# Five pairs of weight blocks by Strassen's seven products in a decoder's memory stage

## What is computed

```python
proj = h @ w_in
qkv, b, a, qm, z = jnp.split(proj, [3 * WIDTH_B, ...])
...
om = mem_attend(qm.reshape(B, T, MEM_HEADS, HEAD_DIM), mem_k, mem_v).reshape(B, T, WIDTH_MEM)
branch = jnp.concatenate([o, om], axis=-1) * jax.nn.silu(z)
return branch @ w_out, new_conv, S.astype(sdt)
```

## Time and profile before

| | before |
|---|---|
| median of 3 runs (their extremes) | 2191.96 us (2190.51 to 2194.2) |
| the profiled execution's own time | 2194.7 us |
| its span, first to last instruction | 2192.7 us |
| PE busy, share of the span | 2154.7 us, 98% |
| DVE, ACT, POOL busy | 938.3, 663.8, 456.4 us |

### The profile page before, as it was taken

The page is one execution under the profiler, slowest core; times in us unless marked ns, Lnnn a source line. Parts: engine busy times, 40 slices in busy tenths (PEclk is TensorE's granted clock), DMA queues, the critical chain, the costliest instruction groups (busy, mean ns, idle before and its releaser), DMA issues.

```text
span 2192.7 us, 46735 instructions
## 1 busy us (share of the span) xinstructions
PE 2154.7 (98%) x19630; PEld 1531.5 (70%) x19630; DVE 938.3 (43%) x2431; ACT 663.8 (30%) x1589; POOL 456.4 (21%) x642
## 2 busy tenths in 40 slices
PE   8999999999999999999999999999999999999998
PEld 6888888888888876544567667676676666665444
DVE  5234354354344444321355555555555233333252
ACT  4122321312222131311234434444344344442101
POOL 0522241242123205000032322322322110020000
PEclk9999999999999999999999999999999999999999
DMA  7412211212221166666012212122110173114451
GB/s 227 154 42 64 81 30 41 78 43 67 58 59 42 35 212 227 213 207 212 13 62 93 70 74 83 67 79 80 60 53 14 40 273 97 39 59 148 136 168 53
DMA packets 210278, 210.99 MB, mean 96 GB/s; under 512 B 14262, under 2 KB 181654, under 8 KB 209151
## 3 DMA queue, kind: packets, MB, share of 16 engines
q1 hardware_dynamic: 198070, 148.27, 22.4%
q0 software_dynamic: 12000, 59.73, 7.1%
HBM read 179.56 MB, written 68.23 MB: 113 GB/s over the span
## 4 chain that ended last, share of the span: by engine, by line
PE 50%; DVE 0%; ACT 0%; issue 0%; POOL 0%; DVEq 0%
PE bank L2088 19%; PE bank L2802 8%; PE bank L3292 7%; PE bank L2146 4%; PE bank L2162 4%; PE bank L2144 2%; PE bank L2154 1%; PE bank L2818 1%; PE bank L2827 1%; PE bank L3270 1%; PE bank L3303 0%; PE bank L2177 0%; PE bank L3199 0%; PE bank L3176 0%; PE bank L2810 0%; PE bank L3186 0%
## 5 line engine op out<-in xcount | busy, mean ns | idle before, releaser
L884 PE MATMUL bank<-arena 128*128 128x256 f32 (+1 forms) x2688 | 631.7, 386 | 0.0
L884 PEld LDWEIGHTS bank<-arena 128*128 128x128 f32 x2688 | 494.5, 190 | 75.3
L2088 PE MATMUL bank<-arena 128*128 128x352 f32 x1296 | 469.2, 474 | 0.1
L2088 PEld LDWEIGHTS bank<-arena 128*128 128x128 f32 x1296 | 214.0, 190 | 58.1 <-ACT arena L2309 0.6
L2802 PE MATMUL bank<-arena 128*128 128x352 f32 x576 | 176.4, 459 | 0.0
L3292 PE MATMUL bank<-arena 128*128 128x512 f32 x360 | 167.5, 599 | 0.0
L2146 PEld LDWEIGHTS bank<-arena 128*128 128x128 f32 x864 | 125.5, 192 | 36.7 <-issue 0.3
L2802 PEld LDWEIGHTS bank<-arena 128*128 128x128 f32 x576 | 106.6, 190 | 53.3
L2162 PEld LDWEIGHTS bank<-arena 32*32 32x32 f32 x7680 | 78.8, 105 | 91.6 <-issue 39.8
L1338 POOL TENSOR_TENSOR arena<-arena 128x272 f32<-128x272 f32 (+1 forms) x48 | 31.5, 656 | 507.6 <-ACT arena L1058 487.6
L2146 PE MATMUL bank<-arena 128*128 128x128 f32 x864 | 131.3, 278 | 0.2 <-ACT arena L2329 0.2
(11 more groups left out here) (426 smaller groups left out, 2720.2 us busy)
## 6 DMA issues: line engine op xcount, KB each, us to landing
arena<-in_w_in_a SPq DMA_DIRECT2D x48, 512.0 KB, 5.1
arena<-in_w_in_b SPq DMA_DIRECT2D x40, 512.0 KB, 4.1
arena<-in_cache_win_k SPq DMA_DIRECT2D x48, 256.0 KB, 5.1
arena<-in_cache_win_v SPq DMA_DIRECT2D x48, 256.0 KB, 3.6
out<-arena SPq DMA_DIRECT2D x40, 256.0 KB, 3.3
arena<-in_w_mem_kv SPq DMA_DIRECT2D x16, 512.0 KB, 8.0
arena<-in_cache_mem_k SPq DMA_DIRECT2D x32, 256.0 KB, 4.1
arena<-in_cache_mem_v SPq DMA_DIRECT2D x32, 256.0 KB, 3.4
```

The lines of the kernel that those rows point to most:

```text
L884: m = nc.tensor.matmul(o[:, 0:hi - lo], w, y, start=k == 0 and i in (0, 1, 3, 5), stop=k == KH - 1, skip_group_check=i in (2, 4, 6))
L2088: m = nc.tensor.matmul(bank[j % 3][:, 0:PART], ring.slots[:, (B1 + b) % RING, k, :], part_in(k, part_), start=k == 0, stop=k == KD - 1)
```

## The change

Blocks 5 to 14 become five pairs (some blocks change places so that pairs fit). For a pair, the two weight blocks are the columns and the two halves of the contraction the rows of a 2 x 2 matrix; a quarter of the tokens (264) and the next quarter make the other matrix. One *task* is one pair with one half of the tokens: seven products of four matmuls of 264 columns each (28 *units*; the plain form has eight such products). There are ten tasks, two a pair. Their 280 units and the eight of block 15's first piece are spread over the 32 turns by `m_at`: 168 over the first 15 turns, 120 over the other 17.

POOL forms the four sums of tokens of each task (264 x 4 columns each, into buffers that the next task overwrites), the four sums of weights of each pair (128 x 4 columns) and one difference of products a task, and the six later gate multiplications stand between them. DVE reads each product out of PSUM (a copy or an addition; two instructions for the seventh), in its turn between `turned(x-1)` and `normed(x)`. ACT's work on products is the silu, in place, of both blocks when a task is done. The buffers lie where five of the `w_out_b` blocks were to lie, so these are loaded when the last product has been read.

```diff
@@ -206,8 +206,8 @@
         c += (s * P, H * E + (HB + s) * P, H * E + 2 * s * P, H * E + (2 * s + 1) * P)[i]
         return w_in_b[0][:, c:c + P]
 
-    M_BLOCKS = [(0, 0), (0, 1), (0, 2), (0, 3), (1, 0), (1, 1), (1, 2), (2, 0), (2, 1), (1, 3), (3, 0), (3, 1),
-                (2, 2), (2, 3), (3, 2), (3, 3)]
+    M_BLOCKS = [(0, 0), (0, 1), (0, 2), (0, 3), (1, 0), (1, 1), (1, 2), (1, 3), (2, 2), (2, 0), (2, 1),
+                (3, 0), (3, 1), (2, 3), (3, 2), (3, 3)]
@@ -2762,15 +2762,57 @@
...
+    WO_LATE = (0, 1, 2, 3, 4)
+    QUART = TOK // 4
+    HALVES = ((0, QUART, 2 * QUART), (2 * QUART, 3 * QUART, 4 * QUART))
+    tk2, tk3, tk4, tk1 = (sb[:, o:o + TOK].rearrange("p (k c) -> p k c", c=QUART)
+                          for o in (WO_B[0], WO_B[3], ZM[0] + TOK, WO_B[2]))
+    ws2, ws1, ws4 = (sb[:, o:o + KH * P].rearrange("p (k c) -> p k c", c=P)
+                     for o in (WO_B[0] + TOK, qs_at, qs_at + KH * P))
+    s1w, u2b, u3b = (sb[:, WO_B[4] + QUART * n:WO_B[4] + QUART * (n + 1)] for n in range(3))
+    tpd, tpv, tpp, tws, ttk, tz = (sem(f"m_{n}") for n in (
+        "product_done", "product_read", "third_less", "weight_sums", "token_sums", "pair_gates"))
+    a_of = lambda t: bank[2 * (t % 2)]
+    c_of = lambda t: bank[2 - 2 * (t % 2)]
+    PAIR0, NPAIRS = 5, 5
+    NTASKS = 2 * NPAIRS
     (p2, pr2d, sc2, scr2, mx2, ex2, nm2, tn2, tr2, pv2, or2, zo2, nct, ncr) = (sem(f"m_{n}") for n in (
         "piece_done", "piece_read", "scores", "scores_read", "max", "exp", "normed", "turned", "turned_read",
         "values", "values_read", "gated", "conv_turned", "conv_read"))
     nco = stored["conv"]
-    NP2 = 3 * len(M_BLOCKS)
+    NP2 = IN_B + 6
     FIRST_M, LAST_M = IN_B + 3, 2
-    beside = lambda x: range(FIRST_M + x * (NP2 - FIRST_M - LAST_M) // (8 * H),
-                             FIRST_M + (x + 1) * (NP2 - FIRST_M - LAST_M) // (8 * H))
-    queries_read = lambda s: 3 * (M_AT[(s, 1)] + 1) - IN_B
+    munits = [("product", t, i, k) for t in range(NTASKS) for i in range(NPROD) for k in range(KH)]
+    munits += [("piece", FIRST_M, 0, k) for k in range(KD)]
+    MID = 6 * NPROD * KH
+    m_at = lambda x: x * MID // 15 if x < 15 else MID + (x - 15) * (len(munits) - MID) // (8 * H - 15)
+    beside = lambda x: munits[m_at(x):m_at(x + 1)]
+    ended_m = lambda x: [(kind, t, i) for kind, t, i, k in beside(x) if k == (KD if kind == "piece" else KH) - 1]
+    block_of = lambda j: j // 3 if j < FIRST_M else len(M_BLOCKS) - 1
+    pair_of = lambda b: (b - PAIR0) // 2
+    def block_home(s, i, cs):
+        return (mq_of(s) if i == 0 else zm_of(s) if i == 1 else zo_of(s, i - 2))[:, cs]
...
@@ -2779,7 +2821,7 @@
                 sp.dma_start(wo_b(k), w_out_b[0][k * P:(k + 1) * P]).then_inc(w_out_in[1], 16)
 
         readout(sp, NG_ - 1, "ot")
-        w_load(range(6))
+        w_load((5,))
         sp.wait_ge(ncr, 6)
...
         sp.wait_ge(or2, 8 * (H - 1))
         w_load(range(9, 11))
         ring.load(sp, B2 + 16)
+        sp.wait_ge(tpd, NPROD * NTASKS)
+        sp.wait_ge(tpv, 8 * NTASKS)
+        w_load(WO_LATE)
...
+        def product(t, i, k):
+            b, half = PAIR0 + t // 2 * 2, t % 2
+            lo, mid, hi = HALVES[half]
+            left, right = (ring.slots[:, (B2 + b + x) % RING, :, :] for x in range(2))
+            if k == 0:
+                if i == 0:
+                    if not half:
+                        ring.wait(pe, B2 + b)
+                        ring.wait(pe, B2 + b + 1)
+                    if t:
+                        pe.wait_ge(tpv, 8 * t - 4)
+                    else:
+                        pe.wait_ge(pr2d, 1)
+                elif i == 1:
+                    if t:
+                        pe.wait_ge(tpv, 8 * t - 2)
+                    else:
+                        pe.wait_ge(pr2d, 2)
+                elif i == 2:
+                    pe.wait_ge(tpv, 8 * t + 1)
+                    pe.wait_ge(tws, 4 * (t // 2) + 2)
+                    pe.wait_ge(ttk, 4 * t + 2)
+                elif i == 3:
+                    if not t:
+                        pe.wait_ge(pr2d, 3)
+                    pe.wait_ge(tws, 4 * (t // 2) + 3)
+                elif i == 4:
+                    pe.wait_ge(tpv, 8 * t + 3)
+                elif i == 5:
+                    pe.wait_ge(ttk, 4 * t + 3)
+                else:
+                    pe.wait_ge(tpv, 8 * t + 5)
+                    pe.wait_ge(tws, 4 * (t // 2) + 4)
+                    pe.wait_ge(ttk, 4 * t + 4)
+            o, w, y = ((a_of(t), left[:, k, :], hT[:, k, lo:mid]),
+                       (bank[1], left[:, KH + k, :], hT[:, KH + k, lo:mid]),
+                       (a_of(t), ws2[:, k, :], tk2[:, k, :]),
+                       (c_of(t), ws4[:, k, :], hT[:, KH + k, mid:hi]),
+                       (a_of(t), right[:, k, :], tk3[:, k, :]),
+                       (bank[1], right[:, KH + k, :], tk4[:, k, :]),
+                       (a_of(t), ws1[:, k, :], tk1[:, k, :]))[i]
+            m = nc.tensor.matmul(o[:, 0:QUART], w, y, start=k == 0 and i in (0, 1, 3, 5),
+                                 stop=k == KH - 1, skip_group_check=i in (2, 4, 6))
+            if half and i in (2, 6) and k == 0:
+                m.then_inc(ring.used, 1)
+            if k == KH - 1:
+                m.then_inc(tpd, 1)
...
@@ -2844,8 +2944,8 @@
             if x:
                 scores(x)
                 turn_probs(x - 1)
-            for j in beside(x):
-                piece(j)
+            for kind, n, i, k in beside(x):
+                product(n, i, k) if kind == "product" else piece(n, (k,))
             if x:
                 values(x - 1)
...
+        def gates(t):
+            half = t % 2
+            act.wait_ge(tpv, 8 * t + 8)
+            for b in (PAIR0 + t // 2 * 2, PAIR0 + t // 2 * 2 + 1):
+                s, i = M_BLOCKS[b]
+                if i:
+                    v = block_home(s, i, slice(HALVES[half][0], min(HALVES[half][2], SEQ)))
+                    m = nc.scalar.activation(v, v, ACT.Silu)
+                if half:
+                    dst = qms[:, s * NS:(s + 1) * NS] if i == 0 else zs[:, HB + s if i == 1 else 2 * s + i - 2, :]
+                    m = nc.scalar.activation(dst, block_home(s, i, slice(SEQ, TOK)), ACT.Silu if i else ACT.Copy)
+            m.then_inc(tz, 1)
...
+                for kind, n, i in ended_m(x):
+                    if kind == "piece":
+                        piece(n)
+                    elif i == NPROD - 1:
+                        gates(n)
...
+        def product(t, i):
+            (s0, i0), (s1, i1) = (M_BLOCKS[PAIR0 + t // 2 * 2 + x] for x in range(2))
+            half = t % 2
+            lo, mid, hi = HALVES[half]
+            a, b, c = (v[:, 0:QUART] for v in (a_of(t), bank[1], c_of(t)))
+            first, second = slice(lo, mid), slice(mid, hi)
+            dve.wait_ge(tpd, NPROD * t + i + 1)
+            if i == 0:
+                after(dve, tpv, 8 * t)
+                nc.vector.tensor_copy(s1w, a).then_inc(tpv, 1)
+            elif i == 1:
+                dve.wait_ge(tpv, 8 * t + 1)
+                if not half:
+                    home_free(dve, s0, i0)
+                nc.vector.tensor_tensor(block_home(s0, i0, first), b, s1w, ALU.add).then_inc(tpv, 1)
+            elif i == 2:
+                nc.vector.tensor_copy(u2b, a).then_inc(tpv, 1)
+            elif i == 3:
+                dve.wait_ge(tpv, 8 * t + 3)
+                nc.vector.tensor_tensor(s1w, c, u2b, ALU.add).then_inc(tpv, 1)
+            elif i == 4:
+                after(dve, tpp, t)
+                nc.vector.tensor_copy(u3b, a).then_inc(tpv, 1)
+            elif i == 5:
+                dve.wait_ge(tpv, 8 * t + 5)
+                if not half:
+                    home_free(dve, s1, i1)
+                nc.vector.tensor_tensor(block_home(s1, i1, first), b, u3b, ALU.add).then_inc(tpv, 1)
+            else:
+                nc.vector.tensor_copy(block_home(s1, i1, second), a).then_inc(tpv, 1)
+                dve.wait_ge(tpp, t + 1)
+                nc.vector.tensor_tensor(block_home(s0, i0, second), a, s1w, ALU.add).then_inc(tpv, 1)
         for t in range(4):
             conv_turned(t)
         dve.wait_ge(pr_, NPB * HB + IN_B)
         top(0)
         for t in range(4, 6):
             conv_turned(t)
-        normed(0, 0)
-        for x in range(1, 8 * H):
-            top(x)
-            turned((x - 1) // 8, (x - 1) % 8)
+        for x in range(8 * H):
+            if x:
+                top(x)
+                turned((x - 1) // 8, (x - 1) % 8)
+            for kind, n, i in ended_m(x):
+                if kind == "product":
+                    product(n, i)
             normed(x // 8, x % 8)
-            outputs((x - 1) // 8, (x - 1) % 8)
...
-        for s in range(H):
+        def weight_sums(p, ns):
+            b = PAIR0 + 2 * p
+            left, right = (ring.slots[:, (B2 + b + x) % RING, :, :] for x in range(2))
+            done = NPROD * (2 * p - 1)
+            for n in ns:
```

(125 more changed lines are left out.)

3 lines of the change are left out of this document (added).

## The result

The changed kernel takes 2198.81 us (median of 8 runs, 2196.68 to 2202.36), the kernel before 2193.12 beside it. The ratio is 1.0028, 95% interval 1.0019 to 1.0036: slower by 0.28%, just outside the 0.2% within which nothing can be told. Forecast were 2192.5 and "no change within 0.2%": the time lies in the range, but the change is larger than that 0.2%. The profiled execution has a span of 2196.4 us, 3.7 more than before.

What follows compares the result with a forecast made beforehand. PE, busy in all 191.00 us of a memory-stage window, was taken as the bound. Saving -17.2, losses +10.8 in the first three pairs and +6.9 in the last four tasks gave +0.5: 2192.5 us, range 2183 to 2202.

Steps and rivals of the forecast that it cites:

- no change within 0.2%: Whole kernel: the forecast case, 2192.5 us, within the 4.4 us a measurement cannot tell from no change; chance 0.43.
- The saving: PE in the memory stage: 240 piece matmuls at 0.591 us become 280 units at 0.445, -17.2 us.
- DVE's order and POOL's hold: Turn ends: product reads and POOL instructions delay the normalising multiplication, +10.8 us in first three pairs, +6.9 in last four tasks.
- The walk's 1.84 at unit 56: Pair's end, followed step by step: multiplication issued inside a token sum, ending at 31.9 us, so PE loses 1.84 us.
- unit 33: Turn end in a pair: multiplication issued inside a token sum; loss 0.6 us, but 1.5 in the first pair.
- unit 28: End of each last-four task: multiplication slips in or awaits a token sum; 1.6 us even, 1.1 odd, 0.67 last.
- The sums' rate: POOL's token sums: 2.43 us for two-token sums, 2.07 for the others, bounds 1.96 and 2.64.
- the rival with sums at 2.64: POOL's token sums at the slow rate: 26 us of losses, +8.8, 2200.8 us; chance 0.23.
- the first rival: Multiplication rarely meets POOL, so only DVE's order costs: -11.5 us, 2180.5, or 2186.5 with half the meetings; chance 0.27.
- Ring loads come a pair ahead, and five fewer transfers stand before them: Loads of input weight blocks in the memory stage: claimed to cost nothing.
- the thinnest cover: ACT behind a finished task: next softmax's multiplication ends near S + 5.3 us, needed at S + 5.6; no cost.
- The five late blocks: Output blocks loaded after the last product: 8.0 us plus about 2, with 5 us of cover left; no wait.

Runs made afterwards that it cites:

- ninth kernel: Changed kernel, four cache copies issued behind the last-but-one pair's weight sums, DVE reading late-ending products behind the normalising multiplication: 2186.88 us, 0.9965 of the kernel before.
- experiment 4: Changed kernel, DVE reading late-ending products behind the normalising multiplication, last four cache copies moved into the DeltaNet stage: 2203.64 us, 1.0045 of the kernel before.
- tenth version: The ninth kernel with ACT's gates of a task that ends with its turn put behind the next turn's exponential: 2180.64 us, 0.9939 of the kernel before.
- eighth experiment: Changed kernel, last four cache copies moved from the memory stage's start to behind the last-but-one pair's weight sums: 2193.99 us, 0.9999 of the kernel before.

## Why the prediction was off by 6 us

- **The saving** (-17.2): right, -17.0.
- **DVE's order and POOL's hold** (10.8 + 6.9): right in mechanism, and in the two sums: 9.7 and 6.6. The walk's 1.84 at unit 56 is what the trace shows. That the sums agree so closely is partly luck: the first pair loses 0.8 at unit 11, where nothing was forecast, and 0.8 in place of 1.5 at unit 33; of the four ends at unit 28, one loses 1.62 and three slip in at 0.66, where 1.6, 1.1, 1.6 and 0.67 were taken. The two work together, not side by side: with the order undone the multiplication is as slow as before (0.934 us on average in the ninth kernel), yet the turns of the first three pairs lose nothing. The Trainium skill (SBUF — State Buffer, "Who interferes with whom") states that a `tensor_scalar` in VectorE's modes with two ports contends with GpSimd, and that the one issued first keeps the shared ports for its whole instruction. The trace agrees for this multiplication: 23 of the 32 began inside a GpSimd instruction, and all of them ended 0.15 to 0.19 us behind it. In which mode it ran no run shows. It is not so for every one-input instruction from SBUF to SBUF: the reciprocal and the maximum began inside a GpSimd instruction 20 times each and took their usual 0.15 and 0.42 us.
- **The sums' rate** (2.43 and 2.07 us): they take 2.25 on average. No wait for sums appeared in the changed kernel; it came, as the prediction feared, once the order was undone (1.9 us, experiments 4, 9 and 10). The measured time is near that of the rival with sums at 2.64 (2200.8), but the sums were not slow: it came out there for another reason. So it is luck, too, that the time lies in the range: the range was drawn for the sums' rate and the first rival, and no rival had the wait that follows here.
- **"Ring loads come a pair ahead, and five fewer transfers stand before them": the step that failed.** It was put at nothing and cost 4.3 us of waiting and 1.7 of clock. Coming a pair ahead is not enough where the load takes 38 us: block 8 is issued at 1770.99, as soon as its slot is free, and wanted at 1804.6. Before, it was issued at 1793.4, landed 22.9 later and was needed only at 1825.2: late already, but hidden. I priced transfers by loads without copies beside them, and left out what GpSimd's queue moves in that time. The eighth experiment shows the step by itself: with four copies moved, the changed kernel goes from 5.7 us over the kernel before to 0.1 over it, with the losses at the turns unchanged (16.6 us). The four are those of the twelve that still ran behind 1766.2, and the packet counts show the load's packets taking turns with theirs.
- **ACT's gates**, "the thinnest cover", put at nothing: in the changed kernel they hide behind DVE's order (over the whole stretch the reciprocal waits 1.6 us for the exponential, in the ninth kernel 7.7). Once that is undone they cost some 4.4 us at the turns (ninth to tenth version, 7.0 to 2.7) and 1.7 of clock behind the longest of these; the medians differ by 6.2.
- **The five late blocks**: right, no wait at the first output unit.

## What to carry to other kernels

When a change makes an engine reach a weight block sooner, look up that load's own time from issue to landing in that stretch, and what every other queue moves then and in packets of what size: a transfer that was late and hidden becomes the wait, and a wait of some us takes the clock with it. Where an in-order engine serves two chains, put the instruction that the busiest engine waits for ahead of those that can wait, before asking how long each one is. Undoing one loss often exposes the next: judge an edit by the waits in its stretch as well as by the total.

## What the hardware showed that I had not expected

- A block load of 512 KB lands in 3.7 to 4 us, and in 37.8 to 50.0 when GpSimd's DRAM-to-DRAM copies (12.46 MB) were issued before it, though the DMA engines are busy for only about half of the time: each 65.5 KB packet of the copies took 2.42 us, and the loads' queue moved one small packet for each of them.
- VectorE's multiplication from SBUF to SBUF ends 0.15 to 0.19 us behind the GpSimd instruction in which it began (23 of 23); its reciprocal and its maximum, begun in the same way, lose nothing (20 each).
- PE's idle 4.1 us (behind 1.6 of another wait) were followed by a granted clock of 0.53 and then 0.79 over ten us, and eleven units took 6.57 us in place of 4.91. In experiment 4, 2.2 us of idle time were followed by 0.66 over five us, and seven units took 4.80 in place of 3.12.
- Four copies (some 8 MB) moved into the DeltaNet stage cost it 14.5 to 18.8 us (first product at 1785.26 and 1789.57 in place of 1770.79).
